# A dense product for three of nine expert blocks, with weights added into a matrix in DRAM

## What is computed

```
q = (hf @ w_query).reshape(-1, 8, 2, 128)
s = einsum('nhpk,hpmk->nhpm', q, sub_keys)          # two scores lists of 128 per head
sv, si = top_k(s, 16)                               # then the best 16 of the 256 pairs:
fv, fpos = top_k(comb, 16)
eid = take_along_axis(cidx, fpos, axis=-1)          # expert number, 0 to 16383
gate = softmax(fv, axis=-1)
a = einsum('phkd,pd->phk', u_table[ex], hx)         # 8 heads x 16 experts = 128 a token
act = gelu(a, approximate=False) * gx
out = einsum('phk,phkd->pd', act, v_table[ex])
```

## Time and profile before

| what | value |
|---|---|
| median of 3 runs (lowest, highest) | 3583.11 us (3578.18, 3589.97) |
| the profiled execution | 3583.99 us |
| its span | 3582.2 us |
| granted TensorE clock, mean | 0.803 |
| bytes moved by DMA | 1251.85 MB, 349 GB/s over the span |
| indirect DMAs issued by POOL | 1056 for u, 1056 for v |

### The profile page before, as it was taken

How to read it: one execution, slowest core, us unless ns; L and a number is a source line. 1 busy time by engine, 2 the same in 40 slices (tenths; PEclk the granted TensorE clock), 3 DMA queues, 4 the chain that set the end, 5 groups by cost and what they waited for, 6 DMA issues and landing times.

```text
span 3582.2 us, 30420 instructions
## 1 busy us (share of the span) xinstructions
PE 2246.2 (63%) x9719; PEld 980.1 (27%) x9719; DVE 2134.7 (60%) x4860; ACT 361.4 (10%) x755; POOL 2292.5 (64%) x2229
## 2 busy tenths in 40 slices
PE   7582895668748888666467777444445444454566
PEld 6472552135413344211124444011011111011111
DVE  2355877665576666575764556766666666665301
ACT  2111241001120122100000010000000000000000
POOL 0123556766677766676766676777777777777665
PEclk9796998789969999788678888776676666767799
DMA  7767868999999999899999999999999999999998
GB/s 233 184 234 246 296 215 311 393 369 400 380 382 404 406 347 355 316 397 377 384 368 378 370 386 367 364 367 376 370 383 369 379 368 374 364 365 356 364 372 308
DMA packets 372669, 1251.85 MB, mean 349 GB/s; under 512 B 37879, under 2 KB 41359, under 8 KB 372495
## 3 DMA queue, kind: packets, MB, share of 16 engines
q0 software_dynamic: 304784, 1109.40, 82.2%
q1 hardware_dynamic: 45551, 96.47, 7.7%
q10 hardware_dynamic: 22176, 44.04, 3.3%
HBM read 1228.70 MB, written 21.67 MB: 349 GB/s over the span
## 4 chain that ended last, share of the span: by engine, by line
POOL 30%; PE 26%; DMA 19%; issue 14%; DVE 6%; another core or an unknown queue 3%; ACT 1%; DVEq 1%; SPq 0%; POOLq 0%; ACTq 0%
POOL v_ring L804 16%; POOL u_ring L787 14%; DMA v_ring<-in_v_table_dram,eidt 13%; PE bank L1701 11%; PE bank L1537 4%; PE bank L1619 4%; DVE u_ring L1340 3%; DMA u_ring<-in_u_table_dram,eid 3%; PE bank L1520 3%; PE bank L1595 2%; DMA u_ring<-in_v_table_dram,eidt 1%; DMA wring<-in_w_ada_dram 1%; POOL u_ring L804 1%; PE bank L1635 0%
## 5 line engine op out<-in xcount | busy, mean ns | idle before, releaser
L1701 PE MATMUL bank<-v_ring,act_x 128*32 128x512 f32 x3984 | 1205.1, 822 | 980.3 <-DMA v_ring<-in_v_table_dram,eidt 879.3
L1340 DVE CUSTOM_DVE_ANT_0 u_ring<-u_ring,h 128x1024 f32<-128x1024 f32 x1056 | 1279.9, 1225 | 899.1 <-DMA u_ring<-in_u_table_dram,eid 719.1
L787 POOL DMA_INDIRECT u_ring<-in_u_table_dram,eid x1024 | 1106.8, 1081 | 530.5 <-issue 301.3
L804 POOL DMA_INDIRECT v_ring<-in_v_table_dram,eidt x996 | 1075.4, 1080 | 565.3 <-issue 253.2
L1701 PEld LDWEIGHTS bank<-v_ring,act_x 128*32 128x32 f32 x3984 | 269.3, 136 | 1829.7 <-issue 1820.9
L1619 PE MATMUL bank<-hbuf,wring 128*128 128x128 f32 (+1 forms) x2048 | 258.8, 281 | 48.4 <-issue 46.6
L1619 PEld LDWEIGHTS bank<-hbuf,wring 128*128 128x128 f32 x2048 | 244.7, 196 | 84.1 <-issue 83.7
L1537 PE MATMUL bank<-zc,dring 128*128 128x384 f32 x496 | 198.1, 527 | 16.9 <-ACT dring L834 13.4
L1520 PE MATMUL bank<-hbuf,wring 128*128 128x384 f32 (+2 forms) x512 | 165.6, 482 | 15.5 <-ACT hbuf L847 10.5
L1363 DVE TENSOR_TENSOR scratch<-bank,mod 128x512 f32<-128x512 f32 x18 | 11.6, 687 | 189.9 <-PE bank L1701 188.6
L1595 PE MATMUL bank<-wring,mixt 128*128 128x512 f32 (+1 forms) x256 | 123.0, 631 | 1.1 <-DMA wring<-in_w_out_dram 1.1
(11 more groups left out here) (225 smaller groups left out, 1621.5 us busy)
## 6 DMA issues: line engine op xcount, KB each, us to landing
u_ring<-in_u_table_dram,eid POOLq DMA_INDIRECT x1024
wring<-in_w_out_dram ACTq DMA_DIRECT2D x16, 1024.0 KB
wring<-in_w_query_dram ACTq DMA_DIRECT2D x16, 1024.0 KB
v_ring<-in_v_table_dram,eidt POOLq DMA_INDIRECT x996
v_ring<-in_w_ada_dram SPq DMA_DIRECT2D x11, 1024.0 KB, 10.7
wring<-in_w_ada_dram SPq DMA_DIRECT2D x10, 1024.0 KB
wring<-in_w_in_dram ACTq DMA_DIRECT2D x10, 1024.0 KB
xr<-in_x_prompt_dram SPq DMA_DIRECT2D x16, 512.0 KB
```

The costliest lines, as they stand in the source:

```text
L787: pool.indirect_dma_start(u_ring[:, n % NU], None, u_table[0], bass.IndirectOffsetOnAxis(ap=col, axis=0)).then_inc(u_in[n % NU], 16)
L804: pool.indirect_dma_start(place, None, v_table[0], bass.IndirectOffsetOnAxis(ap=eidt[:, b % RING, t:t + 1], axis=0)).then_inc(landed, 16)
L1340: dve.tensor_tensor_reduce(u_ring[:, n % NU], u_ring[:, n % NU], h2[:, b % 2], 1.0, 0.0, ALU.mult, ALU.add, dot[:, b % 2, k:k + 1]).then_i ...
L1701: last = pe.matmul(acc[h][j * S:(j + 1) * S, :], act_x[:, i % 2, j, a:a + S], v_place(n)[0][:, h * HALF:(h + 1) * HALF], start=(c == 0), s ...
```

## The change

Blocks 1, 2 and 3 (`DENSE`) no longer gather rows of v. For each of the three a matrix of 16384 experts x 128 tokens lies in DRAM (`w_dram`, 8 MB each).

- **Zeros.** SP writes the three matrices to zero with 24 DMAs of 1 MB (`w_clear`), two a slot in slots 18 to 29. The source is the zeroed tile `act_x`. ScalarE's first spread waits for them.
- **Weights.** For a dense block, `weigh` leaves act in `actd` and computes for each pair the address 128 x expert + token (`waddr`). POOL issues 128 indirect DMAs a block (`put`): each adds one word from each of 128 partitions to its place in the matrix (`compute_op=ALU.add`). They lie in slots 2 to 31 of pass b + 1, four or five a slot, behind the slot's u gathers. Two heads can name the same expert for a token, so every 16th put waits until all earlier ones have landed.
- **The product.** From slot 161 on (`D_AT` = 160) the table is streamed once, in 64 tiles of 1 MB (4 buffers), with the three blocks' weights beside it (3 x 1 MB for four table tiles, two buffers). SP issues these loads. A dense step (`dense`) is one table tile for one block: four f32 products of 128 x 128 with 512 columns. There are 192 steps; with a cost of 3.55 and a room of 7 they go two to a slot, slots 161 to 256. `ACC` gives the blocks three pairs of PSUM banks.
- **The order of v.** Block 0's gathers take slots 32 to 73, three chunks in four slots (`V_AT`). Blocks 4 to 7 and block 8 get theirs behind the loop, after the last u gather (`V_TAIL`, 544 gathers). `V_LAST` is now 132, so from there on the v ring has 12 buffers. Weights and expert numbers of the blocks that wait are kept in tiles that are free by then (`actts`, `eidts`).
- **The plan.** The room is 4.5 up to slot 73 and 6 behind it, for both groups. `finish(0)` moves to slot 76, all others behind the loop.

Core of the diff:

```diff
+DENSE = [1, 2, 3]
+GATHER = [b for b in range(NB + 1) if b not in DENSE]
+VI = {b: i for i, b in enumerate(GATHER)}
+ND = len(DENSE)
+NE = P * P
+WG = 8
+VS = 2
+NVT = NE // (P * VS)
+D_AT = (DENSE[-1] + 2) * NCH
...
+    fill([("dense", i, j, d) for i in range(NWG) for j in range(WG // VS) for d in range(ND)], D_AT + 1, 7)
...
+V0_END = NCH * 7 // 3
+V_AT = {}
+for c_ in range(NCH):
+    V_AT.setdefault(NCH + c_ * 4 // 3, []).append((0, c_))
+V_TAIL = [(b, c) for b in GATHER[1:] for c in range(rows(b) // CH)]
+
+PUT_AT = [[k for k in range(P) if k * (NCH - 2) // P + 2 == c] for c in range(NCH)]
...
+        ACC = {b: ps[2 * i:2 * i + 2] for i, b in ((0, 0), (0, 1), (1, 2), (2, 3), (0, 4), (1, 5), (2, 6), (0, 7), (1, SB))}
...
+            def w_clear(i):
+
+                sp.wait_ge(x_zero, 1)
+                sp.dma_start(w_dram[i // 8].rearrange("(r p x) o -> r p (x o)", r=8, p=P)[i % 8], xflat[:, 0:NE // 8]).then_inc(w_zero, 16)
...
+            def v_load(n):
+
+                if n >= NVP:
+                    sp.wait_ge(d_used, n - NVP + 1)
+                i, j = n // (WG // VS), n % (WG // VS)
+                sp.dma_start(vt[n % NVP], v_table[0].rearrange("(i p j s) d -> i j p s d", p=P, j=WG // VS, s=VS)[i, j]).then_inc(vt_in[n % NVP], 16)
...
+            def put(b, k):
+
+
+                d = DI[b]
+                if k == 0:
+                    pool.wait_ge(wd_ready, d + 1)
+                    pool.wait_ge(w_zero, 16 * 8 * ND)
+                elif k % K == 0:
+                    pool.wait_ge(w_put, 16 * (d * P + k))
+                pool.indirect_dma_start(w_dram[d], bass.IndirectOffsetOnAxis(ap=waddr[:, d, k:k + 1], axis=0), actd[:, d, k:k + 1], None,
+                                        compute_op=ALU.add).then_inc(w_put, 16)
...
-                    for j in range(CH):
-                        if p:
-                            v_fetch(p - 1, c * CH + j)
+                    for b, vc in V_AT.get(p * NCH + c, []):
+                        for j in range(CH):
+                            v_fetch(b, vc * CH + j)
+                    if p - 1 in DI:
+                        for k in PUT_AT[c]:
+                            put(p - 1, k)
...
+                if b in DI:
+
+                    dve.wait_ge(gel_ready, PARTS * (b + 1))
+                    dve.tensor_tensor(actd[:, DI[b]], dot[:, b % 2], gate[:, b % RING].rearrange("p h k -> p (h k)"), ALU.mult)
+                    dve.tensor_scalar(work[:, 0:P], eidf[:, b % 3], float(P), tcol[:, :], ALU.mult, ALU.add)
+                    dve.drain()
+                    dve.tensor_copy(waddr[:, DI[b]], work[:, 0:P])
+                    dve.drain().then_inc(wd_ready, 1)
+                    return
...
+                for s in range(VS):
+                    for h in range(2):
+                        last = pe.matmul(ACC[DENSE[d]][h][:, :], wt[i % 2][:, d, j * VS + s, :], vt[n % NVP][:, s, h * HALF:(h + 1) * HALF],
+                                         start=(n + s == 0), stop=(n == NVT - 1 and s == VS - 1))
```

More of the change, by code:

```diff
@@ L142, in mixer_steps @@
     return out
-COST = {"state": 3, "x": 1.5, "mean": 2, "var": 2, "out": 4, "turn2": 2, "q": 4.2, "s": 1.2, "state_out": 2}
+COST = {"dense": 3.55, "state": 3, "x": 1.5, "mean": 2, "var": 2, "out": 4, "turn2": 2, "q": 4.2, "s": 1.2, "state_out": 2}
 COST_BLOCK = {"in": 0.75, "conv": 1.5, "pool": 0.4}
@@ L208, in build @@
           u_table, v_table, g_final, y_prompt, y_sample, pool_prompt, conv_prompt, pool_sample, conv_sample):
+    w_dram = [nc.dram_tensor(f"weight_scratch{d}", [NE * P, 1], F32, kind="Internal").ap() for d in range(ND)]
     x1_dram = nc.dram_tensor("x1_scratch", [NT, D], F32, kind="Internal").ap()
@@ L371, in build @@
         bada_zero, x_zero = sem("bada_zero"), sem("x_zero")
+        w_zero, wd_ready, w_put, d_used, d_done = (sem(n) for n in ("w_zero", "wd_ready", "w_put", "d_used", "d_done"))
+        wt_in = [sem(f"wt_in{i}") for i in range(2)]
+        vt_in = [sem(f"vt_in{i}") for i in range(NVP)]
         xss, xstd, xn_ready, xt_ps, xt_taken, xs_ready = (
@@ L474, in build @@
                     transfers[s_ + 1].append(("state", step[1]))
+                elif kind == "dense" and step[3] == ND - 1:
+                    n = step[1] * (WG // VS) + step[2]
+                    if n + NVP < NVT:
+                        transfers[s_ + 1].append(("vt", n + NVP))
+                    if n % (WG // VS) == WG // VS - 1 and step[1] + 2 < NWG:
+                        transfers[s_ + 1].append(("wt", step[1] + 2))
+        transfers[D_AT + 1].insert(0, ("dense",))
+        for i in range(ND * 8):
+            transfers[NCH // 2 + 2 + i // 2].append(("zero", i))
+        transfers[V0_END + 4].append(("y", 0))
         for s_, todo in enumerate(steps):
@@ L702, in _ @@
                     h2_load(p + 1)
[L703 to L706, removed]
+            for b in range(1, NB):
+                y_store(b)
+                if b < LAST:
+                    y_load(b + 1)
             sp.wait_ge(x1_stored[SB % 2], 16 * (SB // 2 + 1))
@@ L819, in _ @@
                         pool.drain().then_inc(x_zero, 1)
-            for i in range(S):
-                v_fetch(NB, i)
+            for b, vc in V_TAIL:
+                for j in range(CH):
+                    v_fetch(b, vc * CH + j)
         @block.scalar
@@ L1090, in _ @@
             take_weights(NB)
-            spread(NB, 0)
-            fin_root(LAST)
+            for b, vc in V_TAIL:
+                if vc in SPREAD_AT and (b < NB or vc == 0):
+                    spread(b, SPREAD_AT.index(vc))
+                if vc == 2:
+                    for a in DENSE if b == GATHER[1] else [b - 1]:
+                        fin_root(a)
             fin_root(NB)
@@ L1457, in _ @@
                         dve.drain().then_inc(fold_ready, 1)
-            finish(LAST)
-            finish(NB)
+            for b in range(1, NB + 1):
+                finish(b)
         @block.tensor
@@ L1760, in _ @@
                 for c in range(NCH):
[L1761 to L1764 removed]
+                    if c == 0 and p - 1 in VI:
+                        weights(p - 1)
+                    for v in V_AT.get(p * NCH + c, []):
+                        tokens(*v)
                     for step in steps[p * NCH + c]:
@@ L1792, in _ @@
                             states_out(step[1])
+                        elif kind == "dense":
+                            dense(*step[1:])
             weights(NB)
-            for c in range(NSG):
-                tokens(NB, c)
+            for v in V_TAIL:
+                tokens(*v)
 _INS = ['x_prompt', 'x_sample', 'state_pool', 'state_conv', 'c_prompt', 'c_sample', 'w_ada', 'b_ada', 'g_norm1', 'g_norm2',
```

167 lines of the change are left out of this document (120 added, 47 removed).

## The result

The changed kernel takes 4133.5 us (median of 4 runs, 4120.38 to 4139.24) against 3586.54 for the kernel before beside it: 1.152 times the time, 95% interval 1.149 to 1.156. It is slower by 547 us. The profiled execution took 4120.38 us, with a span of 4118.4.

What follows compares the result with a forecast made beforehand. The prediction saw a transfer-bound loop with POOL's issuing nearly as slow; stages ending at 588, 981, 2137, 3029 and 3070 us, a 781 us tail and 21 us gave a span of 3864, forecast 3865 us, range 3560 to 4250.

Steps and rivals of the forecast that it cites:

- put stage: Slots 66 to 160: 784 indirect DMAs of POOL at 1.37 us plus waits, 1156 us, 12.3 a slot.
- late v gathers: Behind the last u gather: 544 v gathers at 1.435 us each, 781 us, with nothing running beside them.
- slots 32 to 66: Three v gathers a slot in place of four: 393 us, ending at 981 us.
- dense stage: Slots 160 to 257: DMA, PE and VectorE near their limits together, 9.2 us a slot, 892 us.
- put's price: Slots 66 to 160: a put costs POOL a gather's 1.37 us, with bounds of 0.86 and 2.0.
- sign: Slots 66 to 160: the prediction is wrong if puts measure under 0.6 us or over 1.8.
- landing waits: Slots 66 to 160: POOL waits for puts to land 18 times at 4 us, 72 us.
- ring waits: Slots 66 to 160: ten us more for ring waits.
- Rival 2: Slots 66 to 160: a put holds POOL or the queue 2.74 us, total 4390 us; chance 0.12.
- The claim that indirect DMAs, not bytes, are counted: In the passes, removing bytes but not indirect DMAs gains only some 20 us a pass.
- rival 1: Slots 66 to 160 fall to VectorE's pace with cheap puts; total from 3420 up to 3572 us; chance 0.10.

Runs made afterwards that it cites:

- e2: The changed kernel with puts that write in place of adding: 3928.34 us against 4112.55 for the changed kernel beside it; 3839.57 us on another chip.
- b1: The kernel before with v gathers of blocks 1 to 3 cut to one word a row: ratio 0.997 on one chip, 0.993 on another (3541.2 us).
- b_same: The kernel before, unchanged, run again on another chip for its stages: 3557.84 us.
- e5: The changed kernel with the table not streamed, three of 192 dense steps left: 4035.85 us beside 4108.31 for the changed kernel.

## Why the prediction was right, and where it was off

Forecast 3865 us in 3560 to 4250, slower; measured 4133.5. The direction and the mechanism were right: POOL's queue sets the put stage, and the late v gathers come at their full price. But the loss was forecast at 282 us and is 547. The sum, span against span, was 3864 and is 4118. The kernel before stands beside it, cut at the starts of the same u and v gathers.

| step | before | predicted | measured |
|---|---|---|---|
| slot 32 begins | 573 | 588 | 590 |
| slots 32 to 66 | 440 | 393 | 413 |
| slots 66 to 160 | 1154 | 1156 | 1400 |
| slots 160 to 257 | 1128 | 892 | 860 |
| to the last u gather | 74 | 33 | 42 |
| the late v gathers | 192 | 781 | 793 |
| to the end of the span | 21 | 21 | 20 |

The changed kernel loses 601 us in the late v gathers and 246 in the put stage, and wins 268 between slots 160 and 257; the other steps together win 43, which leaves 536 between the spans. The late v gathers and the dense stage were forecast well; the put stage was forecast as no loss at all. Of the 254 us by which the sum fell short, 244 are that stage. The other steps are off by 2, 20, -32, 9, 12 and -1, and that they leave only 10 together is luck.

**The put's price was the term of the wrong size.** The prediction took a gather's 1.37 us for a put, with bounds of 0.86 and 2.0. It is 2.12, beyond the upper one, and makes 384 x 0.75 = 288 us. By its own sign, puts over 1.8 us (without the pause), the prediction was wrong at this step: they measure 1.83 on the mean. The nearest row was chosen by the number of entries that POOL writes, which e2 shows to be right for a plain scatter (0.96 us at the shortest), and the addition, for which no row stood, was put into the upper bound with too little. Against that the landing waits were 3.0 us and not 4 (18 us less), and u and v gathers of the stage took POOL 1.31 us with the pause and not 1.37 (23 less). 288 - 18 - 23 and 2 us less of ring waits (8.3 and not 10) are 245, the 244 of the table but for rounding. Rival 2, dear puts, was half true: POOL's part was dear; the queue's was not. (It names 4230 us as the upper edge of the range, which is 4250.) The software queue needed no more than a DMA share of 0.62 for the stage, near the 0.6 to 0.7 that was forecast.

**The claim that indirect DMAs, not bytes, are counted** is shown from one side by b1, where taking only the bytes out of the kernel before brings 0.3 to 0.7%, and from the other by e1, where taking out 384 puts shortens their stage by 516 us. The prediction had given 20 us a pass for the bytes; passes 2 to 4 took 389, 388 and 382 us in b1_pair against 384, 398 and 384 in b_same. The dense product replaces 384 gathers of 1.37 us of POOL by 384 puts of 2.12. Per block that is 96 us of POOL more, in a queue that the passes had filled already.

**Cheap puts, rival 1, had the wrong threshold.** It said that the loss vanishes at 0.82 us a put. e1 has puts for nothing and is still 3.5% slower than the kernel before on its chip. On the chip of the result, with a stage of 884 us in place of 1400, the span would be 4118 - 516 = 3602 us, still above 3582. This is an estimate, and a low one, since the 884 us come from the chip with the quicker DMA. What the rival left out: without the puts the stage is not at VectorE's 8.4 us a slot but at 9.4, since in pass 2 VectorE waits for the mixer's products, and POOL for VectorE.

**The dense stage** came out at 8.9 us a slot for 9.2, with PE at a granted clock of 0.89 and a DMA share of 0.93; e5 shows that it is within 76 us of VectorE's pace, and that what VectorE waits for there is u rows from the DMA, not PE. **The late v gathers** came at 1.46 us each for 1.435. They are the larger part of the loss, and the prediction had it right: 793 us in which VectorE does 44.

**Slots 32 to 66** took 20 us more than forecast. 31.7 of their 413 us went into slots 64 and 65, where the forecast has 20. The kernel before is as slow there: its slot 64 begins at 982.7 us and its slot 66 at 1013.5, not at the 1007 that the prediction worked out. So 12 of the 20 us are a stretch that the trace of before had shown, and the puts have no part in it. What makes it slow no run shows.

By the Trainium skill, DMA: Bandwidth & Descriptors, in its section on the anatomy of a DMA on the software path, descriptor generation is "small, variable". These rows don't agree for indirect DMAs, if the time that one holds POOL is taken for it: 0.94 us a gather, 1.55 a scatter-add, and in the put stage this is the limit. By the Trainium skill, same page, SWDGE vs HWDGE vs iDMA, VectorE locks GpSimd out of the memory where descriptors are written while it works in its 2-port performance mode. The traces agree in kind: a v gather held POOL 1.09 us on the mean in slots 32 to 66, where VectorE was busy two thirds of the time, and 0.95 in the tail, where it was nearly idle. Whether VectorE was in that mode at those moments, no run shows.

No run tries a version that would beat the kernel before. With a put at 2.12 us, POOL alone would need 573 + (928 + 672) x 1.37 + 384 x 2.12 = 3579 us until it had issued its last, even if it never waited once after pass 0. With the 1.31 us that gathers took in the put stage it would be 3483. These are estimates from the rows above: they leave such a version 3% under the kernel before at most by the second, and nothing by the first.

## What to carry to other kernels

Count what each queue must issue before counting bytes: where one engine issues every indirect DMA and is busy nine tenths of its passes, trading a large gather for a small scatter with addition makes its queue longer, however few bytes the scatter moves. A moved transfer costs its full price where nothing runs beside it, and here that was the larger loss; ask of each resource in each stage, not over the span. And for an operation that no trace shows, the bound above must be as far out as the unlike part (here the addition) might reach.

## What the runs showed of the hardware

- An indirect scatter with addition holds POOL 1.55 us at the shortest (1.83 on the mean beside VectorE); without the addition 0.96 and 1.25. With 64 rows in place of 128 the mean falls by 0.145 us only.
- The landing of a put was waited for 3 us at a DMA share of 0.62.
- An indirect gather of one word a row cost POOL no less than one of 4 KB: 1.175 us against 1.090 on the mean.
- The pace of DMA differed from chip to chip: late v gathers came every 1.33 us on one and every 1.45 to 1.46 on the others, and the kernel before took 3410 us there against 3558 to 3587.
